# Plain mixer: gate-row transfers issued by GpSimd, and weight splits, gate steps and convolutions in another order

## The reference

```python
p = h @ w_in                                     # 1024 x 3088
qk, va, oa, gates, uv = jnp.split(p, ...)        # 1024, 512, 512, 16, 1024 columns
qk = silu(centred_dwconv(qk, conv_w))            # 5 taps along the tokens
g = (gates + gate_b).reshape(..., 4, A_HEADS)    # li_f, f_f, li_b, f_b for 4 heads
h_fwd = mlstm_scan(q, k, v, g[0], log_sigmoid(g[1]))
h_bwd = the same on the flipped sequence with g[2], log_sigmoid(g[3])
ha = rms_norm(h_fwd + h_bwd, head_g) * sigmoid(oa)
u, vb = jnp.split(gelu(uv), 2)
vb = rms_norm(vb by group of 128, v_g)
hb = u * (ws[g] @ vb + bs)                       # mixes the tokens of a chunk of 128
return concatenate([ha, hb]) @ w_out
# mlstm_scan: b = cumsum(lf); m = running max; exp(b_t - b_s + li_s - m_t) weights q.k
```

## Time and profile before

| what | value |
|---|---|
| median of 3 runs | 889.74 us (888.76 to 890.2) |
| the profiled execution's own time | 888.97 us |
| its span, first to last instruction | 887.2 us |
| instructions | 14279 |
| TensorE matmul busy | 869.1 us (98%) |
| VectorE busy | 538.0 us (61%) |
| ScalarE busy | 435.1 us (49%) |
| GpSimd busy | 45.9 us (5%) |
| mean granted TensorE clock | 0.996 |
| this mixer | about 293.5 us to after 404 us of the span |

### The profile page before, as it was taken

How to read it: one execution, slowest core, us unless ns; L and a number is a source line. 1 busy time by engine, 2 the same in 40 slices (tenths; PEclk the granted TensorE clock), 3 DMA queues, 4 the chain that set the end, 5 groups by cost and what they waited for, 6 DMA issues and landing times.

```text
span 887.2 us, 14279 instructions
## 1 busy us (share of the span) xinstructions
PE 869.1 (98%) x5832; PEld 784.6 (88%) x5832; DVE 538.0 (61%) x586; ACT 435.1 (49%) x595; POOL 45.9 (5%) x109
## 2 busy tenths in 40 slices
PE   8999999999999998999999999999999999999997
PEld 7987899999999997888999999989867999999996
DVE  5866554444456759878675555567676775555553
ACT  6566444433434676743654444436465374444431
POOL 1200100000000200320000000003000000000000
PEclk9999999999999999999999999999999999999998
DMA  9823155555456374336675555444601575555511
GB/s 293 302 96 124 42 190 191 179 192 195 157 189 224 97 244 142 141 96 218 198 239 190 189 189 189 136 130 122 216 32 50 191 240 192 188 188 187 190 44 47
DMA packets 98441, 147.68 MB, mean 166 GB/s; under 512 B 4042, under 2 KB 81938, under 8 KB 98402
## 3 DMA queue, kind: packets, MB, share of 16 engines
q1 hardware_dynamic: 97234, 143.11, 49.1%
q0 software_dynamic: 1120, 4.00, 1.5%
q10 hardware_dynamic: 48, 0.02, 0.0%
HBM read 146.05 MB, written 1.05 MB: 166 GB/s over the span
## 4 chain that ended last, share of the span: by engine, by line
PE 91%; DVE 3%; DMA 2%; ACT 1%; POOL 1%; issue 1%; SPq 0%; ACTq 0%; DVEq 0%; POOLq 0%
PE bank L1893 27%; PE bank L1894 27%; PE bank L1895 27%; DMA w_raw<-in_swa_w_in 2%; PE bank L1967 1%; PE bank L2531 1%; PE bank L2554 1%; PE bank L2516 1%; PE bank L2510 1%; PE bank L2095 1%; PE bank L2107 1%; PE bank L2094 1%; DMA x_norm<-arena 1%; DVE w_lo L1189 1%; PE bank L2284 0%
## 5 line engine op out<-in xcount | busy, mean ns | idle before, releaser
L1189 DVE TENSOR_TENSOR w_lo<-w_raw,w_hi 128x2048 fp32r<-128x2048 f32 (+3 forms) x129 | 289.4, 2251 | 151.8 <-ACT w_hi L676 151.6
L1893 PE MATMUL bank<-xT_hi,w_hi 128*128 128x256 f32 x1068 | 304.6, 285 | 4.5 <-DVE w_lo L1189 4.4
L1895 PE MATMUL bank<-xT_hi,w_lo 128*128 128x256 f32 x1068 | 302.8, 284 | 0.0
L1894 PE MATMUL bank<-xT_lo,w_hi 128*128 128x256 f32 x1068 | 302.8, 283 | 0.0
L676 ACT ACTIVATE w_hi<-w_raw 128x2048 fp32r<-128x2048 f32 (+3 forms) x129 | 241.2, 1877 | 91.6 <-PE bank L1895 83.1
L1893 PEld LDWEIGHTS bank<-xT_hi,w_hi 128*128 128x128 f32 x1068 | 204.7, 192 | 9.3 <-DVE w_lo L1189 4.8
L1894 PEld LDWEIGHTS bank<-xT_lo,w_hi 128*128 128x128 f32 x1068 | 204.7, 192 | 1.9 <-issue 0.2
L1895 PEld LDWEIGHTS bank<-xT_hi,w_lo 128*128 128x128 f32 x1068 | 204.6, 192 | 0.2
L1893 PE MATMUL bank<-w_hi,ff_hi 128*128 128x512 f32 x344 | 134.6, 391 | 0.0
L1894 PE MATMUL bank<-w_lo,ff_hi 128*128 128x512 f32 x344 | 134.3, 390 | 0.0
L1895 PE MATMUL bank<-w_hi,ff_lo 128*128 128x512 f32 x344 | 133.9, 389 | 0.0
(11 more groups left out here) (274 smaller groups left out, 799.3 us busy)
## 6 DMA issues: line engine op xcount, KB each, us to landing
w_raw<-in_ffn_w SPq DMA_DIRECT2D x64, 1024.0 KB, 5.3
w_raw<-in_ffn_w_gate_up SPq DMA_DIRECT2D x22, 1024.0 KB, 5.1
w_raw<-in_ab_w_in SPq DMA_DIRECT2D x12, 1024.0 KB, 5.9
w_raw<-in_ffn_w_down SPq DMA_DIRECT2D x11, 1024.0 KB, 4.8
w_raw<-in_swa_w_in SPq DMA_DIRECT2D x5, 1024.0 KB, 11.0
w_raw<-in_swa_w_out SPq DMA_DIRECT2D x4, 1024.0 KB, 7.4
w_raw<-in_ab_w_out SPq DMA_DIRECT2D x4, 1024.0 KB, 4.9
w_raw<-in_c_w_out SPq DMA_DIRECT2D x4, 1024.0 KB, 5.1
```

Of the source, the lines that this page charges most:

```text
L1189: dve.tensor_tensor(view(w_lo, ch), view(w_raw, ch), view(w_hi, ch).bitcast(F32), ALU.subtract).then_inc(S["lo_done"], 1)
L1893: pe.matmul(out, sh, mh, start=first, stop=False)
L1894: pe.matmul(out, sh, ml, start=False, stop=False)
L1895: return pe.matmul(out, sl, mh, start=False, stop=last)
```

## The change

GpSimd issues the four gate transfers, once `g_raw` is written, in place of ScalarE. On ScalarE `spatial_values(1)` stands before the w_hi of c[6] and takes over the wait for c[3]; the w_hi of c[7] and c[8] follow `g_raw` directly; exp and ln stand behind the copies of the first convolved chunk. On VectorE the splits of c[7] and c[8] stand before the wait for the gate rows, conv(0) before `gate_rows`, the copy of the gate columns before conv(2), the split of c[11] behind conv(3), and that of c[12] behind `weighted_scores(1)`. The number of instructions of compute and the arithmetic stay as they are.

```diff
@@ GpSimd
             pool.memset(ab_v1[:, :, :, AD:AD + 1], 1.0).then_inc(S["pads_ready"], 1)
 
+            pool.wait_ge(S["g_raw_ready"], 1)
+            for k in range(4):
+                pool.dma_start(g4[:, k, :], g_raw[4 * k:4 * k + 4, :]).then_inc(S["g4_loaded"], 16)
@@ ScalarE
             high_upto(c[5].index + 1)
             spatial_values(0)
-            act.wait_ge(S["mm_done"], c[3].index + 1)
+            spatial_values(1)
             high_upto(c[6].index + 1)
             act.wait_ge(S["small_loaded"], 64)
             act.wait_ge(S["mm_done"], c[4].index + 1)
             act.activation(g_raw, bank[0][0:16, 0:SEQ], ACT.Identity, bias=gate_b[:]).then_inc(S["g_raw_ready"], 1)
-            act.wait_ge(S["g_raw_ready"], 1)
-            for k in range(4):
-                act.dma_start(g4[:, k, :], g_raw[4 * k:4 * k + 4, :]).then_inc(S["g4_loaded"], 16)
             act.wait_ge(S["pads_ready"], 1)
             act.wait_ge(S["params_ready"], 1)
-            high_upto(c[7].index + 1)
-            spatial_values(1)
-            act.wait_ge(S["g_abs_ready"], 1)
-            step(act.activation(g_w, g_w, ACT.Exp))
-            act.activation(g_w, g_w, ACT.Ln, bias=1.0).then_inc(S["g_ln_ready"], 1)
+            high_upto(c[8].index + 1)
...
                 last.then_inc(S["conv_begun"], 1)
+                if i == 0:
+                    act.wait_ge(S["g_abs_ready"], 1)
+                    step(act.activation(g_w, g_w, ACT.Exp))
+                    act.activation(g_w, g_w, ACT.Ln, bias=1.0).then_inc(S["g_ln_ready"], 1)
                 high_upto(ch.index + 1 + SLOTS)
@@ VectorE
             dve.wait_ge(S["params_ready"], 1)
-            low_upto(c[6].index + 1)
+            low_upto(c[8].index + 1)
...
                                      op1=ALU.min).then_inc(S["g_abs_ready"], 1)
-            low_upto(c[7].index + 1)
+            conv(0)
...
             gate_rows()
-            for i in range(4):
-                conv(i)
-                low_upto(c[min(8 + i, 10)].index + 1)
+            low_upto(c[9].index + 1)
+            conv(1)
+            low_upto(c[10].index + 1)
             dve.wait_ge(S["g_cols_psum"], 1)
             dve.tensor_copy(ab_t.rearrange("p t k h -> p (t k h)"), bank[1][:, 0:32]).then_inc(S["g_cols_ready"], 1)
-            low_upto(c[8].index + 1 + SLOTS)
+            conv(2)
+            conv(3)
+            low_upto(c[11].index + 1)
...
             weighted_scores(1)
+            low_upto(c[12].index + 1)
```

## The result

The changed kernel takes **882.57 us** (median of four runs, 882.02 to 883.04) against 889.74 before: a ratio of 0.9923, with a 95% interval from 0.991 to 0.9935. It is 7.17 us faster by the medians. The profiled execution took 882.92 us instead of 888.97, 6.05 us less.

The account below looks back on a forecast made before the run. TensorE bounds the kernel, held by the stall before projection(8) and its low clock: -5.85, 0 for moved splits, 0 for GpSimd's issues, +0.25, so -5.6; 888.97 becomes 883.4, then 884.1 us as median, range 882.9 to 887.4.

Parts of the forecast that it names:

- The bound: TensorE, busy 869.1 of 887.2 us, stalls before projection(8) for c[8]'s late split, then runs at low clock.
- the first sum: Before and in projection(8): stall 4.16 plus low clock 1.69 gives 5.85 us that the change can win.
- ScalarE and VectorE up to the landing: Splits of c[6] to c[8] fill VectorE's idle time until 327.85, at no cost; c[8] is 10 us early.
- GpSimd's issues: Four gate-transfer issues at 0.61 us each, 321.45 to 323.9, on an otherwise idle engine, costing 0.
- the rival of late gate rows: Gate transfers fall behind c[10]'s and c[11]'s loads, landing 329.5 to 331.5; gain 4.5 to 2.5 us; chance 0.17.
- T: Landing of the last gate transfer, for which VectorE waits with everything behind; taken as 327.9.
- Descriptors shut out: Rival: GpSimd's issues wait for VectorE's splits, landing 334.3 to 336.7; slower, 890.0 to 894.1 us; chance 0.07.
- The order behind T: VectorE's work after the landing, 24.2 us, ends conv(3) at 352.1; spatial mixing at 363.3 fits with 0.3 us spare.
- The stall moved to the mixing: Rival: GpSimd's masks or pow held by VectorE, vb 2 us late; 885.6 to 887.8 us; chance 0.10.
- the +0.25 us: Allowance in the sum for the gate landing coming some tenths later than its 0.3 us of slack allows.
- the 334.05 of the forecast: Gate landing time from which TensorE waits for silu's chain and gate columns as long as for c[8] before.
- it lies 0.77 us below the median of the runs: Last step: profiled 888.97 less 5.6 gives 883.4; its 0.77 us distance to the median makes it 884.1.

Follow-up runs that it names:

- Run 11: Kernel before with 32 matmuls into an unread bank in front of projection(8), filling the stall: 890.23 us, ratio 1.0008.
- Run 9: Changed kernel with 10 small fills on GpSimd ahead of its four gate-transfer issues: 883.14 us, ratio 0.9928.
- run 10: Changed kernel with 26 small fills on GpSimd ahead of its four gate-transfer issues: 888.15 us, ratio 0.9989.
- run 5: Changed kernel with the four gate-transfer issues given back to ScalarE, all orders of the change kept: 884.26 us, ratio 0.9948.
- run 1: Kernel before, unchanged, run again for a second trace: 888.85 us, ratio 0.9995.
- Runs 13 to 15: Kernel before, unchanged, for its third, fourth and fifth traces, one execution each: 889.58, 889.65 and 889.70 us.
- Run 8: Changed kernel with the split of c[12] directly behind that of c[11]: 882.95 us, ratio 0.9931.
- run 4: Kernel before with the four gate transfers issued by GpSimd instead of ScalarE, all orders as before: 888.57 us, ratio 0.9996.
- run 6: Changed kernel with the copy of the gate columns behind conv(2) and conv(3): 884.33 us, ratio 0.9941.
- run 3: Kernel before with c[7] and c[8] split early on ScalarE and VectorE, nothing else changed: 888.36 us, ratio 0.9996.
- run 7: Changed kernel with conv(0) behind the gate rows, where it stood: 885.02 us, ratio 0.9947.
- 12: Changed kernel with decay_rows(0) in the middle of projection(9) instead of behind it: 882.52 us, ratio 0.992.

## Why the prediction was right in its mechanism and too low in its size

**The bound** was read right. The 4.16 us stall for c[8]'s split is gone, the clock between 336 and 350 is 1.00, and the small transposes came 5.93 us earlier where the first sum had 5.85. Run 11, where the stall is filled, shows that the low clock in front of the small transposes comes with the stall.

**ScalarE and VectorE up to the landing.** I had the absolute value at 327.9, it came at 327.62. The three splits cost nothing there. **GpSimd's issues** took 0.51 us each, not 0.61, and hid as said. They landed 1.9 to 3.1 us after their issue, faster than any row that I had (3.9 to 7.0): the rival of late gate rows did not come about, and T was set by VectorE's own splits. Run 9 shows what it would have been like: issued 1.7 us later they needed 4.2 to 4.8 us, behind c[10]'s load. In the changed kernel that load is issued at 323.27, just behind the start of the fourth issue (323.2); in the kernel before it stood at 322.56, since c[6] was split 0.7 us earlier there.

**Descriptors shut out** did not happen either. The Trainium skill's rule in "SBUF — State Buffer", box "DVE blocks DMA", speaks of VectorE in a two-port mode. I had counted it against this edit without a row that shows these splits in such a mode; had it held for them, the issues would have waited until 327.7. The four issues stand at 321.66 to 323.7, beside three splits that run without a break from 320.95 to 327.70, and all had landed by about 326.3. So beside these splits of 128x2048 f32 the issues were not held, and the measurement decides.

**The order behind T.** Conv(3) ended at 351.94 (predicted 352.1), silu started at 352.05 (352.2), the decay exponentials at 355.41 (355.5), the scaling of vb ended at 362.4 (363.0), spatial mixing stood at 363.10 (363.3). **The stall moved to the mixing** in none of the traces of after: GpSimd's masks and pow kept their durations. I put the slack of this chain at 0.3 us; runs 9 and 10 measured 0.8 to 1.1, which makes the +0.25 us that I had added for it too much. The price of a late chain was about right: run 5 lost some 2 us with the absolute value 2.9 us late, run 10 almost the whole gain with 5.0 us. With T = 332.6 in run 10 there is 1.0 us left (1 - 0.9989, times 889.5), so at one for one nothing is left from T = 333.6 on, close to the 334.05 of the forecast. But two errors cancel there: the gain is larger than I had it, and late gate rows cost more than their waits.

**The step that failed** is the last one of the sum, "it lies 0.77 us below the median of the runs": it takes the way from the profiled execution to the median for a constant that both kernels share. Behind it stands that I sized the low clock from one trace, which has a stretch behind the stall and none behind the decay rows. The term for the first stretch, 1.69 us, held: the way to the small transposes is 324.12 to 324.42 us in four of five traces of before, and only run 1 has 0.8 to 1.1 us more. The second stretch, 1.5 to 1.7 us in three of five, was put at nothing.

The miss is 1.57 us before rounding, and it divides like this. Against the profiled execution the sum had 5.6 us and the runs gave 6.05, 0.45 more: 0.25 for a T that was not late, 0.08 up to the small transposes, 0.12 behind them. The other 1.12 us came with the step to the median: the profiled execution of before lay 0.77 us below its median, that of after 0.35 above. For before the traces show why. Runs 13 to 15 stand near the median (889.58 to 889.70). They have the second stretch, which makes the whole 1.4 to 1.5 us longer than in the first trace, and a start that is 0.8 us shorter; together that is the 0.6 to 0.7 us between them. For after it is shown only in part. All its traces have a long start, with a clock of 0.91 over the first 20 us. Run 8, alike but for the place of one split, has the same whole of 335.10 us behind a start of 24.26 us at a clock of 1.00, and that execution took 881.82 us, 1.1 less. Low clock at the start is no mark of either order: runs 4 and 11 have it too, runs 5, 6, 8, 9 and 10 do not.

**What stays open.** The second stretch of low clock behind the decay rows stands in three of five traces of before and in one of three of after. Of the variants, runs 3 and 11 in the old order and 6 and 7 in the new one have it, runs 4, 5, 8, 9, 10 and 12 do not. Whether taking the stall out makes it rarer is not shown: run 11 has no stall and has it all the same. The gain in the medians may hold a part that is of this kind. ScalarE's new places for spatial_values(1) and for exp and ln were not run by themselves. Nothing is gained elsewhere: counted from the first transpose of the token factors, the first pair is 6.10 us apart at the weighted sum of head 0, and what follows takes the same time in both.

**What each part is worth.** Alone in the old order neither the early splits (run 3) nor GpSimd's issues (run 4) give anything. The order without GpSimd's issues gives some 5 us (run 5), and these some 2 us on top. Within the order, conv(0) ahead of the gate rows is worth 2.5 to 3.1 us (run 7) and the gate columns ahead of conv(2) some 2 us (run 6), both with low clock in it; the place of c[12]'s split is worth nothing (run 8).

## What to carry to other kernels

Before you move one late piece of work forward, look at what stands behind it in its queue: here each single move shifted the stall by one projection or left it, and only the whole order let VectorE's chain keep pace with TensorE. If a stall brings a stretch of low clock, read its price from several traces of the kernel and not from one, and do not carry the distance between a profiled execution and its median over to the changed kernel. Small transfers on which an engine waits belong ahead of the next big load in time, not only on a free queue. And when you move their issue to an idle engine, ask which of the two gains you get: here it was the time on the queue that was freed (run 5).

## What the runs showed of the hardware

Stretches of the lower clock level, some 3.4 or 6.7 us long, come and go between executions of one kernel at the same places: behind the 4 us stall, behind the decay rows (matmuls over 4 rows), and at the start. What one costs is about half of what falls on matmuls: 1.5 to 1.7 us for 3.4 to 3.5 us, 3.3 us for the 6.7 in run 6, 2.4 us for the 6.7 in run 1, of which 1.8 fell into idle time. The start took 24.78 to 25.46 us in the seven traces with a clock of 0.91 there and 24.26 to 24.55 in ten of the eleven with 1.00 (25.36 in the first trace of before). A wait of 0.47 us ahead of the decay rows went with 6.7 us of low clock (run 6).

A transfer of 4 KB that is issued just behind a 1 MB load waits for it, whichever engine issues it: 4.65 us for the last one in the kernel before (ScalarE), about 4.5 and 4.7 for two in run 4 and 4.2 to 4.8 for four in run 9 (GpSimd), against 2.3 to 2.4 us for the two ahead of the load in run 4 and 1.9 to 3.1 us in the changed kernel, where all four issues begin ahead of it.
